# Block 0's last products ahead of block 1's, three half tiles of block 0 at a stage's start, and the forget gate tile by tile

## The reference, cut to what matters

```python
for l in range(2):                                            # first block
    x = x + 0.5 * swiglu(rms_norm(x, ffn1_norm[l]), ...)      # FFN_A
    z = rms_norm(x, mix_norm[l]) @ w_in[l]                    # MIX
    f = lb + (1.0 - lb) * jax.nn.sigmoid(f_logit)             # forget gate
    k = 1.0 - f;  g = jnp.log(f);  b = jnp.cumsum(g)          # running sum, runs of 64 tokens
    ...
    x = x + merged @ w_mix_out[l]                             # M_OUT
    x = x + cross_attention(rms_norm(x, xattn_norm[l]), ...)  # X_Q .. X_O
    x = x + 0.5 * swiglu(rms_norm(x, ffn2_norm[l]), ...)      # FFN_B
x = rms_norm(x, final_norm)
for l in range(2):                                            # second block
    x = x + 0.5 * g1 * swiglu_2(modulate(rmsnorm(x), sh1, sc1), ...)   # FFN_C
    proj = modulate(rmsnorm(x), sh2, sc2) @ w_in[l]           # Z_QI ..
    ...
    x = x + g2 * (o @ w_out[l])                               # Z_O
    x = x + 0.5 * g3 * swiglu_2(modulate(rmsnorm(x), sh3, sc3), ...)   # FFN_D
```

## Time and profile before

| what | value |
|---|---|
| median of 3 runs | 2989.89 us |
| profiled execution, its own time | 2989.78 us |
| its span | 2987.7 us |
| TensorE busy | 2817.1 us (94%) |
| VectorE busy | 1976.3 us (66%) |
| ScalarE busy | 1374.4 us (46%) |
| mean granted TensorE clock | 0.977 of full speed |
| DMA | 564.43 MB, mean 189 GB/s |

### The profile page before, as it was taken

One profiled execution on the slowest core, in us unless ns is written; L12 is line 12 of the kernel. 1 busy time (PEld: TensorE's weight loads), 2 busy tenths in 40 slices (PEclk: granted clock), 3 DMA queues, 4 the chain that ended last, 5 costly groups with the idle time before them and its releaser, 6 DMA issues.

```text
span 2987.7 us, 37668 instructions
## 1 busy us (share of the span) xinstructions
PE 2817.1 (94%) x16040; PEld 2449.9 (82%) x16040; DVE 1976.3 (66%) x2205; ACT 1374.4 (46%) x1550; POOL 224.4 (8%) x197
## 2 busy tenths in 40 slices
PE   6999899999999998999999998989989989899999
PEld 5878899998887877999997886867868878687787
DVE  6666885655666666876555666666866666668644
ACT  5444445444444444445454444444644444346443
POOL 0000330000000000330000000003000000030000
PEclk9999999999999999999999999999999999999999
DMA  7654333445666644333445665653257666432454
GB/s 272 250 213 169 127 128 132 154 160 204 253 242 247 250 183 169 129 127 134 162 159 210 260 251 225 251 195 127 86 197 261 239 246 240 183 127 89 166 187 151
DMA packets 82039, 564.43 MB, mean 189 GB/s; under 512 B 9072, under 2 KB 10576, under 8 KB 15952
## 3 DMA queue, kind: packets, MB, share of 16 engines
q1 hardware_dynamic: 66272, 465.47, 42.7%
q0 software_dynamic: 15600, 96.55, 8.5%
HBM read 560.86 MB, written 1.12 MB: 188 GB/s over the span
## 4 chain that ended last, share of the span: by engine, by line
PE 75%; DVE 15%; ACT 5%; issue 2%; DMA 2%; POOL 2%; SPq 0%; DVEq 0%; ACTq 0%; POOLq 0%
PE ps L304 68%; DVE ring_lo L298 4%; ACT w_hi L291 2%; DMA ring<-stream 2%; PE ps L593 1%; POOL qk L1671 1%; PE ps L942 1%; DVE e L667 1%; PE ps L406 1%; DVE e L465 1%; POOL rope_a L1667 1%; DVE e L470 1%; DVE x L431 0%; PE ps L1071 0%; PE ps L1097 0%
## 5 line engine op out<-in xcount | busy, mean ns | idle before, releaser
L298 DVE TENSOR_TENSOR ring_lo<-ring,w_hi 128x2048 fp32r<-128x2048 f32 x438 | 1012.2, 2313 | 567.8 <-ACT w_hi L291 567.2
L291 ACT ACTIVATE w_hi<-ring 128x2048 fp32r<-128x2048 f32 x438 | 836.8, 1911 | 382.7 <-PE ps L304 304.8
L304 PE MATMUL ps<-w_hi,h_hi 128*128 128x512 f32 (+1 forms) x1920 | 732.9, 382 | 11.9 <-DVE ring_lo L298 10.8
L304 PE MATMUL ps<-w_hi,h_lo 128*128 128x512 f32 (+1 forms) x1920 | 719.7, 375 | 0.0
L304 PE MATMUL ps<-ring_lo,h_hi 128*128 128x512 f32 (+1 forms) x1920 | 719.4, 375 | 0.0
L304 PE MATMUL ps<-h_hi,w_hi 128*128 128x256 f32 x1488 | 434.9, 292 | 25.6 <-DVE ring_lo L298 25.4
L304 PEld LDWEIGHTS ps<-w_hi,h_hi 128*128 128x128 f32 x1920 | 365.9, 191 | 80.3 <-issue 19.7
L304 PE MATMUL ps<-h_lo,w_hi 128*128 128x256 f32 x1488 | 425.6, 286 | 0.0
L304 PE MATMUL ps<-h_hi,ring_lo 128*128 128x256 f32 x1488 | 425.5, 286 | 0.0
L304 PEld LDWEIGHTS ps<-w_hi,h_lo 128*128 128x128 f32 x1920 | 365.6, 190 | 65.1
L304 PEld LDWEIGHTS ps<-ring_lo,h_hi 128*128 128x128 f32 x1920 | 366.3, 191 | 61.6 <-issue 1.4
(11 more groups left out here) (331 smaller groups left out, 3102.1 us busy)
## 6 DMA issues: line engine op xcount, KB each, us to landing
ring<-stream SPq DMA_DIRECT2D x438, 1024.0 KB, 4.8
e<-ada POOLq DMA_DIRECT2D x77, 1024.0 KB, 6.2
rows<-mod_rows POOLq DMA_DIRECT2D x18, 512.0 KB, 5.6
rows<-gain_rows POOLq DMA_DIRECT2D x8, 512.0 KB, 5.7
val<-c_row POOLq DMA_DIRECT2D x4, 512.0 KB, 4.6
x<-x_in SPq DMA_DIRECT2D x4, 256.0 KB, 7.1
mem<-mem_t SPq DMA_DIRECT2D x1, 1024.0 KB, 16.1
out_t<-x SPq DMA_DIRECT2D x4, 256.0 KB, 2.0
```

The lines of the kernel that those rows point to most:

```text
L291: nc.scalar.activation(w_hi[:, p % HIGHS, :], ring[:, p % RING, :], ACT.Copy).then_inc(S.w_hi_ready, 1)
L298: nc.vector.tensor_tensor(ring_lo[:, p % RING, :], ring[:, p % RING, :], w_hi[:, p % HIGHS, :].bitcast(F32), ALU.subtract).then_inc(S.w_lo ...
L304: mm = nc.tensor.matmul(out, a, b, start=start and n == 0, stop=stop and n == 2, skip_group_check=group)
```

## The change

TensorE's products stay the same in number and shape; their order changes, and with it the places of `flip_x`, `high`, `low` and the small work of the crossings.

- End of an FFN: block 1's second half of chunk 10 is split (two k before block 0's last down product, two after it); both down products of block 0 come ahead; `flip_x` of the next stage comes behind everything. ScalarE does the next stage's first `high` and the first two squares (`ahead`) before it copies block 1's last chunk. VectorE does block 1's low part (`within`) inside the crossing, behind `next_low` (the next stage's first tile), the second add and the variance. The last two side products are done together in chunk 9.
- Start of an FFN: `first_three` instead of `first_pair`: block 0 over tiles 0, 1 and half of 2's work, with `flip_x` of block 1 between, then block 1.
- `out_pairs` and Z_O: all of block 0 ahead of most of block 1; M_KV1: the two `flip_x` come later.
- Second block: gain first (`gained`), then scale and shift in one instruction.
- Forget gate: per tile, each `forget(n)` ahead of a `low`; logarithm and running sum in four parts; the two memsets on POOL.

```diff
+        def cross_act(act, n, base, p, late, ready=None, three=True, first=True):
...
+            if first:
+                sq(0)
+                sq(1)
...
+            tile_high(0)
             sq(2)
             sq(3)
             if not late:
                 rstd_act(act, n, 1)
+            if three:
+                tile_high(1)
             h_high(act, n, 2, base)
             h_high(act, n, 3, base)
...
+            if not three:
+                tile_high(1)
...
+            def next_low():
+                if tail is not None:
+                    low(dve, p + 2)
+            def within():
+                if tail is not None:
+                    last_low(dve, tail, 1)
...
             else:
-                for b in range(2):
-                    add(2 * b)
-                    add(2 * b + 1)
-                    if b == 1:
-                        tile_low(0)
-                    variance(dve, n, b)
-                    rstd_dve(dve, chain, n, b)
-                    scaled(2 * b)
-                    scaled(2 * b + 1)
-                    h_low(dve, n, 2 * b, base)
-                    h_low(dve, n, 2 * b + 1, base)
-            tile_low(1)
+                add(0)
+                next_low()
+                add(1)
+                gained(0)
+                variance(dve, n, 0)
+                within()
+                rstd_dve(dve, chain, n, 0)
+                scaled(0)
+                scaled(1)
+                h_low(dve, n, 0, base)
+                h_low(dve, n, 1, base)
+                add(2)
+                tile_low(0)
+                add(3)
+                gained(1)
+                variance(dve, n, 1)
+                rstd_dve(dve, chain, n, 1)
+                scaled(2)
+                scaled(3)
+                if three:
+                    tile_low(1)
+                h_low(dve, n, 2, base)
+                h_low(dve, n, 3, base)
+                if not three:
+                    tile_low(1)
...
+        def first_three(pe, p, n, base, banks, done):
+            for b in range(2):
+                for k in range(KD):
...
+                if b == 0:
+                    mm.then_inc(done, 1)
+                    flip_x(pe, n, 1, base)
+                    pe.wait_ge(S.w_lo_ready, p + 3)
+                mm = half_pair(pe, p + 2, 0, (banks[0] + 2, banks[1] + 2), h2, b)
+            mm.then_inc(S.tile_done, 1)
...
+            for half in range(2):
...
+                mm = part(0, half, 0)
+                if half == 0:
+                    part(0, 0, 1).then_inc(S.tile_done, 1)
+            mm.then_inc(S.out_done, 1)
+            part(1, 0, 0)
+            part(1, 1, 0).then_inc(S.out_done, 1)
+            part(0, 1, 1).then_inc(S.tile_done, 1)
+            part(1, 0, 1).then_inc(S.tile_done, 1)
+            between()
+            part(1, 1, 1).then_inc(S.tile_done, 1)
...
+            down(last - 1, 0, p + 2)
             flip(last, (0,))
+            half_pair(pe, p + 1, 1, (2 * (last % 2), 2 * (last % 2) + 1), h2, 1, range(2))
             pe.wait_ge(S.g_ready, nth(S.g_ready, (CHUNKS + 1) * f + last + 1))
+            pe.wait_ge(S.w_lo_ready, p + 4)
+            down(last, 0, p + 3)
+            half_pair(pe, p + 1, 1, (2 * (last % 2), 2 * (last % 2) + 1), h2, 1, range(2, 4)).then_inc(S.tile_done, 1)
+            down(last - 1, 1, p + 2, (0,))
             flip(last, (1,))
+            down(last - 1, 1, p + 2, (1,)).then_inc(S.tile_done, 1)
+            pe.wait_ge(S.g_ready, nth(S.g_ready, (CHUNKS + 1) * f + last + 2))
+            down(last, 1, p + 3).then_inc(S.tile_done, 1)
             if after:
                 after()
...
+            last_high(0)
+            silu(last, 1)
+            tile_high(3 * last)
+            if ahead:
+                ahead()
+            last_high(1)
...
             out_pairs(pe, M_OUT, 0, h2, S.merged, 0, lambda: None)
-            flip_x(pe, 2, 0, 0)
             project(pe, M_KV1, 6, (mem_hi, mem_lo))
-            flip_x(pe, 2, 1, 0)
+            flip_x(pe, 2, 0, 0)
-            project(pe, M_KV1 + 1, 7, (mem_hi, mem_lo))
+            project(pe, M_KV1 + 1, 7, (mem_hi, mem_lo), middle=lambda: flip_x(pe, 2, 1, 0))
...
+            low(dve, MIX + HIGHS)
+            low(dve, MIX + 1 + HIGHS)
+            def forget(n):
+                part = hk[:, 2 * n:2 * n + 2, :]
+                dve.wait_ge(S.evac_done, nth(S.evac_done, 3 + n))
+                chain(nc.vector.tensor_scalar(part, part, 1.0, None, ALU.add))
+                chain(nc.vector.reciprocal(part, part))
...
             for n in range(4):
+                forget(n)
+                low(dve, MIX + 2 + n + HIGHS)
             low(dve, MIX + 6 + HIGHS)
...
+            running(0)
+            running(1)
             low(dve, MIX + 7 + HIGHS)
+            running(2)
+            running(3)
             low(dve, MIX + 8 + HIGHS)
```

323 lines of the change are left out of this document (177 added, 146 removed).

## The result

The changed kernel took 3040.7 us, median of 4 runs (3031.4 to 3045.2), beside 2990.2 us for the kernel before: 1.0164 times as long, 95% interval 1.0139 to 1.0189. Run again later on another chip it took 3035.9 us (3027.4 to 3041.8), ratio 1.0149, 1.0129 to 1.0169. I had forecast 3011 us, range 2981 to 3034: the direction was right, the size was not, and the time lies outside the range.

What follows compares the result with a forecast made beforehand. TensorE was taken as the bound, through its own work, waits and slow clock. From 2989.8 us, the terms without clock gave -1.0 and the clock charge +22.8: 3011.6, told as 3011 us, 8-in-10 range 2981 to 3034.

Steps and rivals of the forecast that it cites:

- M_OUT to X_Q: M_OUT's crossing, twice: a 5.0 us wait before M_KV1's second tile, X_Q's tile 2.0 late; +12.2 us in all.
- X_O: From X_O to FFN_B, twice: the next stage's first `low` and the first add move 5.5 us later; +7.6 us.
- Z_O to FFN_D: From Z_O to FFN_D's first down product, twice: add starts earlier, `flip_x` waits 0.1 instead of 3.95 us; -13.8 us.
- FFN_C to Z: End of FFN_C, twice: the 6.59 us wait becomes 10 but starts 4 us earlier; +0.3 us each without clock.
- FFN_D to FFN_C: From FFN_D's end into the next FFN_C: almost no change, -0.1 us without clock.
- the loads are late too: Rival, 10%: the fifth tile of seven FFNs comes 2.7 us later each, +19 us, giving 3030 us.
- forget gate: In MIX, twice: waits of 3.44 and 9.25 us give way to new waits of 3.3 us; -27.4 us with clock.
- ends of FFNs: Seven FFN ends before a crossing: TensorE waits 4.2 or 5.2 us for block 1's g_lo; +18.6 us without clock.
- starts of FFNs: FFN starts: the fifth tile's load starts 2.7 us later; a separate cost only in the first FFN, +1.8 us.
- the products of block 1 are ready in time: Rival, 14%: at FFN ends block 1's last chunk comes within TensorE's 4.2 us, seven waits go; 2965 us at best.
- The clock: Across the kernel, matmuls behind the longer new waits run at half clock: 22.8 us charged, bounds 0 and 30.

## Why the prediction was wrong

The forecast was a sum of stretches, each followed to a common point. Here are its waits beside the same stretches of the table above, changed kernel less kernel before (us):

| stretch, waits only | forecast | measured, measured again |
|---|---|---|
| MIX, both layers | -18.8 | -19.3, -19.6 |
| M_OUT to X_Q, both | +12.2 | +11.2, +11.2 |
| X_O to FFN_B's first down, both | +9.3 | +9.6, +9.0 |
| FFN_B to FFN_A's first down | +7.5 | +7.4, +7.2 |
| FFN_A to MIX, both | +5.8 | +7.4, +7.3 |
| FFN_B to final norm to FFN_C's first down | +3.5 | +6.2, +3.1 |
| first FFN | +1.8 | +2.3, +2.4 |
| kernel's end | +1.3 | +0.9, +0.9 |
| **Z_O to FFN_D's first down, both** | -12.1 | -4.6, -4.7 |
| **FFN_C to Z, both** | +0.6 | +6.5, +6.5 |
| **FFN_D to FFN_C's first down** | -0.1 | +5.9, +5.8 |
| whole kernel | +11.0 | +33.8, +30.0 |

Three stretches hold 19 of the 19 to 23 us that are missing; these are the steps that failed.

- *Z_O to FFN_D*, 7.5 us. I listed the new waits rightly (three of 1.7 to 1.9, in the trace 1.16, 1.73 and 1.54, and 0.92) beside old ones of 3.95 and 2.13, which differ by about a microsecond, and yet wrote -7.1 and -5.0 from following the work to the first down product. The direct count of the trace is -1.4 and -1.1 of waits there and -2.2 for the g_lo behind it. The kernel with this order alone gained 5.4 us.
- *FFN_C to Z*, 6 us. I wrote that 6.59 become 10 but start 4 us earlier, +0.3. They became 9.97, and nothing started earlier, since the new wait of 4.94 stands where the 4.58 stood; it is +3.3 twice.
- *FFN_D to FFN_C*, 6 us. Half of it is the wait for the first g_lo: 3.94 and 3.83 us, where I had 0.7 to 1.2 from a load of 4.8 to 6 us. The load took 7.99 and 7.86 us beside POOL's, and 2.4 us of side products stood in g_lo's way too. The rival *the loads are late too* had the late start of the load, not its length.

By parts instead of places, each with its share of the clock, beside what the runs gave (us):

| term | forecast | measured |
|---|---|---|
| forget gate | -27.4 | -26.6 alone |
| Z_O to FFN_D | -13.8 | -5.4 alone |
| ends of FFNs | +18.6 + 16.1 | +29.9 (beside the two above) |
| X_O and M_OUT | +19.8 + 6.7 | +23 to +28 (taken out of the whole) |
| starts of FFNs | +1.8 | +16 alone, +24 to +28 taken out of the whole |
| sum | +21.8 | +45 to +51 |

The rows of this second table don't cut exactly as the forecast did: the third tile's waits (3.1 us each in my figures) stood in its terms for X_O and the ends, and the runs count them under the starts.

- *Forget gate*: right, in mechanism, size and inner sum.
- *M_OUT to X_Q*: right in place and size of the waits (5.0 and 2.0 forecast, 5.02 and 2.00 measured), wrong in what could undo them: a `low` in front of the first add holds 3.2 us of it.
- *X_O*: the sum of the waits was right. Half of what I put down to the `low` ahead of the first add belongs to the new FFN start.
- *Ends of FFNs*: the waits in front of block 1's last product were right (4.2 and 5.2 forecast, 3.87 and 4.94 measured), and the total was about right because too much clock (16.1, where some 6 are left) stood beside too few waits (18.6, where the trace has 24); that is luck. The rival *the products of block 1 are ready in time* I put aside because `next_low` is written ahead of the second add; the run with g_lo ahead of both shows that the order as written was worth about 30 us in the whole, some 18 of them waits at the ends.
- *Starts of the FFNs*: "Only in the first FFN, where nothing else moves, is there a cost" treats the start as a question of the load. The third tile is wanted 24 matmuls earlier, and its split isn't there: 2.91 us where it stands alone, which I had blamed on the crossings.
- *The clock*: +10.8 net was forecast, +22.1 and +8.5 measured in two executions. What it was in the other runs can be told only roughly. The mechanism was right: behind the wait of 3.87 us the granted clock is 0.50, 1.2 GHz, with TensorE busy. The length of the last wait alone does not decide it (below). Of the 30 us between the forecast and the measured median 19 to 23 are waits; the rest is slow clock, of which two executions of the same kernel differ by 14 us.

What would have shown it beforehand: to add up, for each stretch, the waits that I myself expected and compare them with the old ones. By that check neither Z_O's -13.8 nor FFN_C's +0.3 could have stood. What stays open: why the start costs 8 to 12 us more inside the change than alone. The length of the loads at FFN_C's two starts explains some 6 us in the first trace of the changed kernel and some 3 in the second; the clock is the likely carrier of the rest, and no run isolates it.

## What to carry to other kernels

Work out a step that moves waits twice: along the chain, and as a sum of old and new waits in the same stretch; where the two differ, the chain has lost something. When a consumer is moved forward, follow each of its inputs back through every queue (here `high` behind squares, then `low`), not only the one that is said to be late. A load whose length depends on what another queue moves beside it has two prices, and a shift of a few microseconds picks one (4.8 or 8.0 us here, 0.78 or 3.94 us of wait). And in a queue without pauses the order of what stands before the goal changes nothing; only an entry that blocks it for a signal from elsewhere is worth moving.

## What the hardware showed that I had not expected

Waits of nearly the same length leave different clocks behind. Windows of the changed kernel (length, busy time of each engine, PEclk, DMA share, GB/s), behind waits of 3.87, 2.92 and 2.58 us:

```profile
222.50:228.00 5.50, 5.50 (x14) 4.23 (x15) 1.89 (x5) 0.00 (x0) 0.00 (x0) 0.50 0.06 25
...
741.50:745.00 3.50, 3.50 (x16) 2.88 (x17) 1.68 (x7) 2.16 (x4) 0.00 (x0) 1.00 1.00 364
...
942.20:945.00 2.80, 2.80 (x7) 2.22 (x8) 2.38 (x4) 1.77 (x5) 0.00 (x0) 0.50 0.03 6
```

In the kernel with the new starts alone, two waits of 2.91 and 2.92 us at the same place of FFN_B and FFN_A:

```profile
734.20:738.00 3.80, 3.80 (x17) 3.11 (x18) 1.99 (x7) 2.16 (x4) 0.00 (x0) 1.00 1.00 370
...
931.30:935.00 3.70, 3.70 (x10) 2.99 (x11) 1.89 (x7) 2.16 (x4) 0.00 (x0) 0.61 1.01 427
```

So a rule by length, as I used it (1.5 us behind 3.44, nothing behind 2.52), gives a mean at best, and a kernel with many such waits can spread: the changed one did by 14 us in both sets of four runs, the kernel before by 5 to 11 in sets of 7 to 13. The Trainium skill (TensorE: Matmul & The Clock Gate, "What's actually happening") calls the number of slow matmuls at a kernel's start "run-variable" for one and the same kernel; the two executions with 97.2 and 83.6 us of slow clock agree, here for the whole kernel.

A VectorE copy can take far longer beside POOL. In the changed kernel, and in every kernel here with the new forget gate, the copy of 8 columns at MIX's start ran beside POOL's memset; before, it ran alone in 0.17 us:

```profile
243.67 1.37 DVE L1458 COPY lb_now<-lb 128x8 f32<-128x8 f32 x1
```

```profile
242.33 2.67 POOL L1769 MEMSET a_hg<- 128x3072 f32 x1
```

The copy starts 1.3 us after the memset and ends with it, at 245.0. A copy of 1024 columns later took 1.80 us beside a POOL product that started first, 0.69 before. The prediction had the memsets at nothing because "nobody waits for them"; here it cost no time, since VectorE had time in hand. The Trainium skill (SBUF — State Buffer, "SBUF: two separate sides") says that VectorE, in some of its modes, and GpSimd share a pair of ports as an exclusive lock for a whole instruction; the trace agrees with it for copies.
